# Moving the T sums of the way up from GpSimd to VectorE, for all units but the three plain ones

## The reference, cut to what matters

```
h2 = RMSNorm(x) * (1 + scale2(c)) + shift2(c)
x  = x + gate2(c) * (relu(h2 @ w_up)^2 @ w_down)      # w_up 1024 x 4096, w_down 4096 x 1024, float32
```

## Time and profile before

| | |
|---|---|
| runs | 1298.1, 1299.65, 1299.98 us |
| profiled execution | 1299.35 us, its span 1297.6 us |
| PE busy | 1273.4 us, 98% |
| PE weight load busy | 1246.0 us, 96% |
| DVE busy | 812.8 us, 63% |
| ACT busy | 577.2 us, 44% |
| POOL busy | 183.9 us, 14% |
| way up | from 615 to 951 us of the span |

### The profile page before, as it was taken

One profiled execution on the slowest core, in us unless ns is written; L12 is line 12 of the kernel. 1 busy time (PEld: TensorE's weight loads), 2 busy tenths in 40 slices (PEclk: granted clock), 3 DMA queues, 4 the chain that ended last, 5 costly groups with the idle time before them and its releaser, 6 DMA issues.

```text
span 1297.6 us, 24740 instructions
## 1 busy us (share of the span) xinstructions
PE 1273.4 (98%) x10221; PEld 1246.0 (96%) x10221; DVE 812.8 (63%) x1221; ACT 577.2 (44%) x998; POOL 183.9 (14%) x182
## 2 busy tenths in 40 slices
PE   6999999999999999999999999999999999999997
PEld 5999999999998999999999999999999999999996
DVE  7611446664334655447798877677678975688874
ACT  5412324444344533336865555555563434334252
POOL 2000100000000122222333333232310000000021
PEclk9999999999999999999999999999999999999999
DMA  9998422222222543545345553544498666776533
GB/s 314 319 289 280 146 66 67 66 80 82 71 67 75 176 128 111 152 124 153 100 125 174 174 165 125 166 132 142 148 340 260 225 202 220 213 240 195 183 126 101
DMA packets 239596, 211.59 MB, mean 163 GB/s; under 512 B 17185, under 2 KB 220837, under 8 KB 234605
## 3 DMA queue, kind: packets, MB, share of 16 engines
q1 hardware_dynamic: 238620, 209.66, 51.1%
q10 hardware_dynamic: 865, 0.36, 0.1%
HBM read 161.97 MB, written 49.04 MB: 163 GB/s over the span
## 4 chain that ended last, share of the span: by engine, by line
PE 91%; DVE 2%; SPq 2%; DMA 1%; ACT 1%; issue 1%; POOL 1%; DVEq 0%; POOLq 0%; ACTq 0%
PE psum L580 29%; PE psum L581 28%; PE psum L582 28%; PE psum L638 2%; PE psum L804 1%; PE psum L792 1%; PE psum L781 1%; DMA ada_p<-in_w_ada_dram 1%; SPq L2206 1%; POOL st L2132 1%; DMA ff_scratch<-st 1%; SPq L2173 1%; DVE b_lo L1829 1%; DVE xl L1792 0%; PE psum L936 0%
## 5 line engine op out<-in xcount | busy, mean ns | idle before, releaser
L580 PE MATMUL psum<-xh,b_hi 128*128 128x264 f32 x908 | 257.2, 283 | 2.2 <-DVE b_lo L1829 1.9
L582 PE MATMUL psum<-xh,b_lo 128*128 128x264 f32 x908 | 257.7, 284 | 0.0
L581 PE MATMUL psum<-xl,b_hi 128*128 128x264 f32 x908 | 256.3, 282 | 0.0
L580 PE MATMUL psum<-dh,e_hi 128*128 128x264 f32 x896 | 254.9, 285 | 0.0
L581 PE MATMUL psum<-dl,e_hi 128*128 128x264 f32 x896 | 253.9, 283 | 0.0
L582 PE MATMUL psum<-dh,e_lo 128*128 128x264 f32 x896 | 253.7, 283 | 0.0
L580 PE MATMUL psum<-h_hi,w_hi 128*128 128x384 f32 (+1 forms) x624 | 207.8, 333 | 1.5 <-issue 1.5
L581 PE MATMUL psum<-h_lo,w_hi 128*128 128x384 f32 (+1 forms) x624 | 201.5, 323 | 0.0
L582 PE MATMUL psum<-h_hi,w_lo 128*128 128x384 f32 (+1 forms) x624 | 201.3, 323 | 0.0
L580 PEld LDWEIGHTS psum<-xh,b_hi 128*128 128x128 f32 x908 | 170.4, 188 | 3.0 <-DVE b_lo L1829 2.5
L581 PEld LDWEIGHTS psum<-xl,b_hi 128*128 128x128 f32 x908 | 170.5, 188 | 0.0
(11 more groups left out here) (315 smaller groups left out, 2418.1 us busy)
## 6 DMA issues: line engine op xcount, KB each, us to landing
down_raw<-in_w_down_dram SPq DMA_DIRECT2D x72, 512.0 KB, 5.5
dr<-ff_scratch SPq DMA_DIRECT2D x28, 1056.0 KB, 8.1
up_raw<-in_w_up_dram SPq DMA_DIRECT2D x76, 256.0 KB, 3.6
ff_scratch<-st SPq DMA_DIRECT2D x64, 264.0 KB, 3.3
ada_p<-in_w_ada_dram SPq DMA_DIRECT2D x8, 2048.0 KB, 9.9
ff_scratch<-st SPq DMA_DIRECT2D x32, 396.0 KB, 3.7
w_raw<-in_w_in_dram SPq DMA_DIRECT2D x22, 512.0 KB, 4.9
gates_scratch<-g_out SPq DMA_DIRECT2D x16, 528.0 KB, 3.2
```

The costliest lines, as they stand in the source:

```text
L580: mm(out, whi, rhi, start=first, stop=False)
L581: mm(out, whi, rlo, start=False, stop=False)
L582: return mm(out, wlo, rhi, start=False, stop=last)
```

## The change

The T sums of the sixteen up units are made by DVE. T3 stands in the unit's own turn 6 behind its `up_product`; T1 and T2 stand in turn 0 of the next unit and T4 in turn 1, each time behind that turn's `block_lo`. After the last unit they stand in turns 0 and 1 of the way down, ahead of `down_product`. The plain units' sums stay on GpSimd. SP's, ACT's and PE's instructions are the same and in the same order.

```diff
+            def t_sum(v, x):
+
+                if UNITS[v][0] == "plain":
+                    return
+                sl = slice(UNITS[v][2][0], UNITS[v][2][-1] + 1)
+                dve.wait_ge(x_done, 4 * v + {T3: 2, T1: 3, T2: 3, T4: 4}[x])
+                if x != T1:
+                    dve.wait_ge(t_done, 4 * v + {T3: 0, T2: 2, T4: 3}[x])
+                a, b = {T1: (st_12, st[:, X11]), T3: (st[:, X22], st_12), T2: (st[:, X22], st[:, T1]), T4: (st[:, T2], st[:, X21])}[x]
+                tt(st[:, x][:, sl, :], a[:, sl, :], b[:, sl, :], ALU.subtract).then_inc(t_done, 1)
...
                 if kind == "up" and i >= 2:
                     up_product(n, v, i, ts)
+                if kind == "up" and i == 6:
+                    t_sum(v, T3)
+                last_unit = v - 1 if kind != "down" else N_UNITS - 1
+                if last_unit >= 0 and (i == 0 if kind != "down" else n == N_UP):
+                    t_sum(last_unit, T1)
+                    t_sum(last_unit, T2)
+                if last_unit >= 0 and (i == 1 if kind != "down" else n == N_UP + 1):
+                    t_sum(last_unit, T4)
...
-            for e, (n, ts) in enumerate(TURNS):
-                kind, v, i = STEPS[n][:3]
-                if kind == "plain" and i == 2:
-                    t_sum(v, T1)
-                if kind == "up" and i == 6:
-                    t_sum(v, T3)
...
+            for v in range(PLAIN):
+                for x in (T1, T3, T2, T4):
+                    t_sum(v, x)
```

More of the change, by code:

```diff
@@ L2122, in t_sum @@
             def t_sum(v, x):
[L2124 to L2128, removed]
+                sl = slice(UNITS[v][2][0], UNITS[v][2][-1] + 1)
+                order = (T1, T3, T2, T4)
+                pool.wait_ge(x_done, 4 * v + {T1: 2, T3: 4, T2: 4, T4: 4}[x])
                 if x in (T2, T4):
```

## The result

The changed kernel took 1300.77 us in the median (20 runs), the kernel before 1298.81 us in as many runs on the same chip: ratio 1.0017, interval 1.0011 to 1.0023. A later comparison gave 1.0022 (1.0013 to 1.0031). So it is about 2 us slower; 1302.0 was forecast.

A forecast was written before the change was run, and what follows sets the result against it. PE, busy 98% of the span, was taken to bound the kernel. Terms 0.0 + 0.56 + 0.83 + 1.14 = 2.5 us on the profiled 1299.35 us led to a forecast of 1302.0 us, range 1299.2 to 1304.4.

The forecast's parts named there:

- DVE's load: DVE over the way up: rises by some 15 us over 330 us, costing PE nothing in the ten last units.
- the lead in the ten last units: In the ten last units b_lo comes 5 us or more ahead of PE's need, hiding DVE's added load.
- T2's moment: When T2 is known, which SP's send and the two loads behind it wait for: 1.40 us later on DVE.
- B: Second two-half unit, near 717 us: T2 1.40 us later less b_lo's lead of 0.84, +0.56 us.
- A: First two-half unit: PE's wait at 680 goes but returns through a later load near 685; net 0.0, bounds -1.3 and +0.5.
- C: Third two-half unit, near 748 us: T2 1.40 us later less b_lo's lead of 0.57, +0.83 us.
- D: Into the way down: dr lands 1.40 us later, less the first e_lo's lead of 0.26, +1.14 us.
- The late T4: Last unit's T4 on DVE near 969.7, its send and loads about 5 us later; taken as 0, bounds 0 and 3.
- rival 2: Slower: late T4 delays SP's send and loads, overrunning the 0.8 us lead at 980 us; 1304.5 us, chance 0.14.
- Rival 1: The lead holds: B, C and D cost 0.5 us or less each; 1299.5 to 1300.5 us, chance 0.20.
- rival 3: Faster: DVE reaches T2 no later than POOL, loads go up to 1.2 us earlier; 1297.5 us, chance 0.10.

The follow-up runs named there:

- experiment 3: Changed kernel with the sums of units 3, 5 and 7 left on GpSimd, the other 13 units' on VectorE: 1300.11 us, ratio 1.0006 against the kernel before.
- Experiment 1: Changed kernel with SP's sends of non-plain units' results issued behind that turn's loads: 1297.77 us, ratio 0.9989 against the kernel before; repeated, 1298.62 us, 0.9995.
- 4: Only the sums of units 3, 5 and 7 on VectorE, all others on GpSimd as in the kernel before: 1301.00 us, ratio 1.0009.
- 5: Changed kernel with T1 and T2 taken ahead of the turn's weight sum and b_lo on DVE: 1299.17 us, ratio 1.0001 against the kernel before.
- 6: Kernel before, with SP's sends of units 3, 5 and 7 held until the b_lo two steps on: 1305.56 us, ratio 1.0049.
- experiment 7: Kernel before with the first dr load's second half issued later: 1301.19 us, one run; then the kernel before unedited for a second trace: 1297.73 us.

## Why the prediction was right, and where it was not

**DVE's load, right in its effect, too high in size.** 52 long sums at 0.70 us are 36.6 us (forecast 36.8), `b_lo<-s_sum` fell by 70.2 - 44.6 = 25.6 us (forecast 26). But the load rose by 6.4 us of busy time and not by the 15 of the prediction. Another weight sum that had run beside GpSimd (L1816) fell from 948 to 691 ns, 4.1 us over its 16, and instructions in a row overlap, since the next one starts 0.61 us into one of 0.69, so a sum adds less busy time than its length. What hides the rest is the lead in the ten last units, by experiment 3. The Trainium skill, SBUF — State Buffer, Who interferes with whom, was cited for that contention, with its rule that whoever comes second is blocked for the other's whole instruction. The changed trace agrees (0.70 us with POOL idle), and the trace before agrees closely:

```profile
708.57 1.84 DVE L1829 TENSOR_TENSOR b_lo<-s_sum,b_hi 128x512 fp32r<-128x512 f32 x1
```

This `b_lo` started 0.58 us behind POOL's T2, which ended at 709.86, and ended at 710.41, 0.55 later. T2 itself had started 0.03 us behind a weight sum on DVE that kept its 0.69 us, and took 1.87 us where T4, which started with DVE idle, took 1.33. Of these 26 us only 1.48 at the wait at 680 were PE's; part of it came back as the wait at 679.61, the rest as the one at 685.34.

**T2's moment, right.** At B it ended 37.0 us after the common point (710.20 - 673.20), before 709.86 - 674.51 = 35.35; 1.65 later, of which 0.23 is PE's own shift from A: 1.42, forecast 1.40.

**A, +0.23, forecast 0.0.** The weight sum came at 683.99, that is 685.30 on the other trace's clock, forecast 685.26; PE began the step 0.09 late. The other 0.14 came in the next step. Experiment 1 shows the alternative that I had as its lower bound, -1.3: without the queue, -0.95.

**B, +0.73, and C, +0.72; forecast 0.56 and 0.83.** In each, PE starts the waiting step 0.61 late and the next another 0.11 to 0.12: the matmul after a wait takes 0.39 us where the others take 0.28. That start-up was missing in my terms. C's lead was 0.57 in the trace I read, but 0.80 in the second trace of the same kernel, and 1.40 - 0.80 is the 0.6 measured. So A, B and C together are 1.68 us, forecast 1.39, and experiments 1, 3, 4, 5 and 6 show that they come through the send.

**D, 0.0, forecast +1.14: wrong.** The step that failed is "I add the whole 1.40 to its landing". This is the load of `w_down` ahead of `dr` on SP, in the kernel before, then both in the changed one:

```profile
934.70 0.60 SPq L2338 DMA_DIRECT2D down_raw<-in_w_down_dram  x1
```

```profile
936.49 0.60 SPq L2346 DMA_DIRECT2D down_raw<-in_w_down_dram  x1
937.20 1.76 SPq L2355 DMA_DIRECT2D dr<-ff_scratch  x2
```

Against PE the load of `w_down` went 1.4 us later, as foretold, but `dr` only 0.1 us later (264.00 us after the common point in place of 262.22, less PE's shift of 1.68). In the kernel before `dr` had been issued 1.4 us behind the end of that load's issue, so there was room for the queue's delay, and the 1.40 never reached `dr`. And ACT waited less:

```profile
944.01 2.06 ACT L1363 ACTIVATE dh<-dr 128x1056 fp32r<-128x1056 f32 x2 [3.31 <-DMA dr<-ff_scratch]
```

937.20 to 944.01 us is 6.8 us, in place of 8.0. By experiment 7 the kernel before can have 6.7 as well; so I had also taken one execution's late landing, and the lead of 0.26 us that it left, for a property of the kernel; in the next execution it was there 1.3 us earlier. Even a landing after 8.0 us would have cost nothing here, as 0.1 us is less than 0.26. The logic of the lead held when the landing was really late. What makes a landing 6.7 or 8.0 us stays open: in the twelve traces that issue both halves together it took 5.4 to 8.1 us, and the two above 7 us have their last T2 on GpSimd, as three of the shorter ones have. Whether the place of the sums has a part in it isn't shown.

**The late T4, a weaker rival 2, partly right.** Here it is on DVE, then its send and the load of `dr` behind it on SP:

```profile
968.90 0.70 DVE L1893 TENSOR_TENSOR st<-st 128x528 f32<-128x528 f32 x1
```

```profile
969.63 0.87 SPq L2364 DMA_DIRECT2D ff_scratch<-st  x2
970.55 10.17 SPq L2346 DMA_DIRECT2D down_raw<-in_w_down_dram  x7
980.82 1.86 SPq L2355 DMA_DIRECT2D dr<-ff_scratch  x2
```

T4 ended at 969.60, that is 970.9 on the clock of the trace before, where about 969.7 was forecast; PE's shift of 1.7 is in it. PE did not wait near 980, where I had looked, but at 1001 for `dl`, 0.4 and 0.5 us in two traces: not the `w_down` loads were short of lead but the `dr` load, which I had not followed. It was issued 307.6 us after the common point, before 978.17 - 674.51 = 303.7; 1.7 of the 4.0 us are PE's shift, 2.3 the queue's. In experiment 3 T4 is as late, but the load was there 7.3 us after its issue in place of 8.8, and PE did not wait, nor did it in experiment 5, where T4 is on DVE too; this part of the loss hangs on a few tenths of a microsecond. By the common clock the wait at 1001 us made PE 0.65 us later (0.76 in the second trace). With it the trace's sum is 1.68 + 0.65 = 2.33, all of the 2.3 us.

So 2.5 us was forecast and 2.3 measured in the trace, but the agreement flatters: 1.39 for A to C was 1.68, 1.14 at D was 0, and the 0.65 at 1001 us I had put at 0. That the error at D nearly cancels those at the other places is luck. Against the page: PE's waits of the way up are 2.9 against 1.9 us, as foretold. Rival 1 (the lead holds) described D, rival 3 nothing: DVE came to T2 later than POOL.

## What to carry to other kernels

When an instruction moves to a faster engine, compare when its result is known, not how long it takes: here it took 0.71 in place of 1.87 us and was ready 1.4 us later, since it joined a queue. Look in the issuing engine's queue at what stands behind the wait for it; putting loads ahead of sends that nobody is in a hurry for turned a loss of 2.3 us into a gain of 1. A lead or a landing time read from one trace is one draw: before a term rests on a few tenths of a microsecond, read it in a second one.

## What the runs showed of the hardware

- PE's shifts against a common matmul repeat within 0.05 us over the way up between executions of one kernel (three kernels, two traces each), while the stretch before it varied by 2.3 us (672.9 to 675.2 us).
- A load of two times 1056 KB, issued the same way, was there 6.7 or 8.0 us later in two executions of one kernel.
- A wait of 1.77 us of PE was followed by 3.5 us at granted clock 0.52, which cost some 1.6 us, nearly as much as the wait. Waits of 1.34, 1.35 and 1.41 us in the same trace were not. So a stall may cost more than its length; this is one case.
- A `b_lo` that started beside a T sum on GpSimd ended 0.55 us behind that sum's end (710.41 against 709.86), and a T sum that started 0.03 us behind a weight sum on DVE took 1.87 us in place of 1.33: of two such instructions the second one waits.
